# SSD stage of a decoder trunk: each group's scan placed between the half tiles of the following group's projection

## What is computed

```python
u = h @ w_in_a[l]                                     # z | x B C | dt
xbc, conv_new = causal_conv(u[..., D_INNER:D_INNER + CONV_DIM], ...)   # 4 taps, then silu
dt = softplus(dt_raw + dt_bias); A = -exp(a_log)
acum = cumsum(dt * A)                                 # within a chunk
decay_ls = exp(where(causal, acum[l] - acum[s], -inf))
cb = einsum('bclgn,bcsgn->bcgls', C, B)
y_diag = einsum('bcgrls,bcsgrp->bclgrp', cb * decay_ls, x * dt)
states = einsum('bclgn,bclgrp->bcgrpn', B, x * dt * decay_end)
# states are carried over the chunks: s = s * chunk_decay + states
y_off = einsum('bclgn,bcgrpn->bclgrp', C, prev) * exp(acum)
y = rmsnorm((y_diag + y_off + d_skip * x) * silu(z))
```

## Time and profile before

| what | value |
|---|---|
| median of three executions | 3522.46 us (3512.46 to 3524.99) |
| profiled execution | 3522.89 us, its span 3521.2 us |
| PE, DVE, ACT, POOL busy | 3233.1, 1475.4, 1153.1, 269.7 us |
| the chain that ended last | PE 88%, DVE 7%, ACT 2% |
| SSD groups (L1195 of the first to the end of the last) | 637 to 1228 us |

### The profile page before, as it was taken

One profiled execution on the slowest core, in us unless ns is written; L12 is line 12 of the kernel. 1 busy time (PEld: TensorE's weight loads), 2 busy tenths in 40 slices (PEclk: granted clock), 3 DMA queues, 4 the chain that ended last, 5 costly groups with the idle time before them and its releaser, 6 DMA issues.

```text
span 3521.2 us, 55459 instructions
## 1 busy us (share of the span) xinstructions
PE 3233.1 (92%) x22296; PEld 2958.1 (84%) x22296; DVE 1475.4 (42%) x2112; ACT 1153.1 (33%) x1615; POOL 269.7 (8%) x364
## 2 busy tenths in 40 slices
PE   6999996998888898998999999999897878899997
PEld 5899996777777786798999879999896666899996
DVE  4444325656565512325443344443432052444423
ACT  3433323433333332224332223332212242333322
POOL 0000000212221210000000000000001201100000
PEclk9999997999989998999999999999998997999998
DMA  6333221222222233322232233222331601223221
GB/s 199 123 89 89 86 87 53 74 70 66 62 62 62 74 97 108 114 84 66 83 89 89 73 107 103 86 86 88 97 90 38 233 27 51 67 86 87 88 88 52
DMA packets 444922, 305.93 MB, mean 87 GB/s; under 512 B 12517, under 2 KB 415645, under 8 KB 444701
## 3 DMA queue, kind: packets, MB, share of 16 engines
q1 hardware_dynamic: 421780, 231.03, 22.4%
q0 software_dynamic: 19744, 69.48, 5.8%
q10 hardware_dynamic: 3328, 4.47, 0.4%
HBM read 282.73 MB, written 22.20 MB: 87 GB/s over the span
## 4 chain that ended last, share of the span: by engine, by line
PE 88%; DVE 7%; ACT 2%; issue 1%; DMA 1%; ACTq 0%; POOL 0%; SPq 0%; DVEq 0%; POOLq 0%
PE PS L916 64%; PE PS L985 5%; PE PS L962 2%; PE PS L1107 2%; PE PS L1119 1%; PE PS L1236 1%; PE PS L1080 1%; PE PS L1058 1%; DVE yT L1430 1%; DVE rb L1415 1%; PE PS L1238 1%; PE PS L1097 1%; PE PS L1169 1%; PE PS L1248 1%; PE PS L1371 1%
## 5 line engine op out<-in xcount | busy, mean ns | idle before, releaser
L916 PE MATMUL PS<-hH,whi 128*128 128x272 f32 x4048 | 842.7, 289 | 16.4 <-DVE hL L1426 7.7
L916 PE MATMUL PS<-hH,wlo 128*128 128x272 f32 x4048 | 840.2, 289 | 0.0
L916 PE MATMUL PS<-hL,whi 128*128 128x272 f32 x4048 | 837.1, 288 | 0.0
L1411 DVE TENSOR_TENSOR wlo<-raw,whi 128x1024 fp32r<-128x1024 f32 (+2 forms) x401 | 488.8, 1219 | 794.9 <-ACT whi L510 787.4
L510 ACT ACTIVATE whi<-raw 128x1024 fp32r<-128x1024 f32 (+2 forms) x401 | 413.1, 1030 | 756.8 <-PE PS L916 669.2
L916 PEld LDWEIGHTS PS<-hH,whi 128*128 128x128 f32 x4048 | 639.7, 189 | 18.7 <-issue 17.1
L916 PEld LDWEIGHTS PS<-hL,whi 128*128 128x128 f32 x4048 | 639.0, 189 | 0.0
L916 PEld LDWEIGHTS PS<-hH,wlo 128*128 128x128 f32 x4048 | 634.3, 190 | 0.0
L916 PE MATMUL PS<-H,whi 128*128 128x272 f32 x1984 | 412.3, 289 | 5.8 <-DVE L L1817 2.5
L916 PE MATMUL PS<-H,wlo 128*128 128x272 f32 x1984 | 412.1, 289 | 0.0
L916 PE MATMUL PS<-L,whi 128*128 128x272 f32 x1984 | 410.4, 288 | 0.0
(11 more groups left out here) (323 smaller groups left out, 3536.9 us busy)
## 6 DMA issues: line engine op xcount, KB each, us to landing
raw<-in_w_ffn_gu SPq DMA_DIRECT2D x176, 512.0 KB, 3.7
kvr<-in_cache_mem_kv POOLq DMA_DIRECT2D x32, 1024.0 KB, 5.5
raw<-in_w_in_a SPq DMA_DIRECT2D x57, 512.0 KB, 3.7
raw<-in_w_ffn_down SPq DMA_DIRECT2D x64, 448.0 KB, 3.2
rawm<-in_w_mem_kv SPq DMA_DIRECT2D x32, 512.0 KB, 4.4
raw<-in_w_ffn_down SPq DMA_DIRECT2D x32, 512.0 KB, 3.4
raw<-in_w_out_a SPq DMA_DIRECT2D x24, 512.0 KB, 3.6
raw<-in_w_in_b SPq DMA_DIRECT2D x20, 512.0 KB, 3.6
```

What stands on the lines that cost most here:

```text
L916: mm = pe.matmul(PS[:, bank + h, 0:HT], w[:, slot, k * P:(k + 1) * P], x[:, h * HT:(h + 1) * HT], start=first and w is whi and x is hi_k, ...
L1411: dve.tensor_tensor(wlo[:, slot, 0:nk * P], src, whi[:, slot, 0:nk * P].bitcast(F32), ALU.subtract).then_inc(s["w_lo"], 1)
```

## The change

- Projection and scan get banks of their own: units use banks 0 and 1 (first and second half of the columns), the scan banks 2 to 7. A unit is now two half tiles of 24 matmuls (`half(g, j, h)`), each with its own full and free semaphores (`ph0`, `pf0`; `w_mm`, `pf1`).
- A period of group g runs units 4 and 5 of g and then the scan of g; between its steps stand the eight half tiles of units 0 to 3 of group g+1. ACT, DVE, POOL and SP have the work that belongs to them (evacuation, first tap, weight splits, taps, conv rows, loads) at matching places.
- The x, B and C tiles get a second set of buffers (`XB`), used by odd groups. The loop becomes: group 0, three turns of two groups, group 7 without a next one.
- Units 0 to 3 of group 0 stand around the dt chain on PE, DVE and ACT.
- A store of `nst` is awaited by DVE just ahead of the next use and not by POOL right behind the store. The scan has a single bank for the spread decays (before: two in turn), and the second new-state product stands behind head 3.
- Behind the loop PE waits for the last output sums (`y_read`) too.

The core of the diff:

```diff
+        XB = [[xbc[:, ti, :] for ti in range(4)], [rb[:, :], dtx_all[:, :], M1[:, 2 * NG - 2, :], M1[:, 2 * NG - 1, :]]]
...
+                    def half(g, j, h):
+                        if h == 0:
+                            pe.wait_ge(s["w_lo"], gx(g, 6, d.u0 + j + 3))
+                        pe.wait_ge((s["pf0"], s["pf1"])[h], gx(g, 6, j + 1))
+                        slot = (d.u0 + j) % 2
+                        for k in range(KD):
+                            for w, x in ((whi, hH), (whi, hL), (wlo, hH)):
+                                mm = pe.matmul(PS[:, h, 0:HT], w[:, slot, k * P:(k + 1) * P], x[:, k, h * HT:(h + 1) * HT],
+                                               start=k == 0 and w is whi and x is hH, stop=k == KD - 1 and w is wlo)
+                        mm.then_inc((s["ph0"], s["w_mm"])[h], 1)
...
-                            products((d.u0 + j) % 2, KD, 0, hH_of, hL_of, 2 * POS[j], True, True).then_inc(s["w_mm"], 1)
...
+                        ahead(0, 0)
                         spread(0)
...
+                        ahead(0, 1)
...
+                        state_rows(0)
+                        ahead(1, 0)
                         spread(1)
+                        ahead(1, 1)
                         head(0)
                         spread(2)
+                        ahead(2, 0)
                         head(1)
                         spread(3)
                         state_rows(1)
+                        ahead(2, 1)
...
                         new_states(0)
                         head(2)
+                        ahead(3, 0)
                         head(3)
...
+                        new_states(1)
+                        ahead(3, 1)
...
                         decay(0)
+                        ahead(0)
                         pair_decay(0)
                         state_rows(0)
                         decay(1)
+                        ahead(1)
                         pair_decay(1)
                         decay(2)
                         pair_decay(2)
                         decay(3)
                         state_rows(1)
+                        ahead(2)
                         pair_decay(3)
...
                         masked(0)
+                        if not last:
+                            conv(ahead, 0, st)
+                            history(ahead, 2)
                         seg(1)
+                        if not last:
+                            unit(g, 9)
                         masked(1)
                         seg(2)
+                        if not last:
+                            conv(ahead, 1, st)
+                            history(ahead, 3)
                         masked(2)
                         seg(3)
+                        if not last:
+                            unit(g, 10)
                         masked(3)
...
                         new_states(0)
+                        if not last:
+                            conv(ahead, 2, st)
                         new_states(1)
```

More of the change, by code:

```diff
@@ L1157, in _, with period, ahead @@
+                    for j in range(2, 4):
+                        half(0, j, 0)
+                        half(0, j, 1)
                     pe.wait_ge(s["hist_copied"], 1)
-                    d = ph["ssd"]
-                    e0 = list(n.ev)
-                    def group(g):
+                    pe.wait_ge(s["alb_sub"], 1)
+                    def period(g, last=False):
+                        xt = lambda ti: XB[parity(g)][ti]
+                        def ahead(j, h):
+                            if not last:
+                                half(following(g), j, h)
@@ L1788, in _ @@
[L1788 removed]
+                        assert last or st.n == VE, st.n
+                    periods(dve, period)
                     d = ph["qm", 0]
```

610 lines of the change are left out of this document (335 added, 275 removed).

## The result

The changed kernel takes 3425.3 us (median of four executions, 3424.1 to 3426.6); the kernel before took 3517.7 us beside it. The ratio is 0.9739, with a 95% interval of 0.972 to 0.9758. The profiled execution took 3424.1 us, with a span of 3422.4. The prediction was 3419, range 3410 to 3446.

What follows compares the result with a forecast made beforehand. PE was taken to bound the kernel, with idle or half-speed time to recover. Seven periods of 65.6 us, the opening and the last scan put the restart 104.7 us earlier: 3522.9 - 104.7 = 3418.2, stated as 3419, range 3410 to 3446.

Steps and rivals of the forecast that it cites:

- The period: Group loop: scan start to scan start takes 65.6 us instead of 78.5, from 64.7 + 0.2 + 0.7.
- The floor from rows at full clock: PE's shortest possible period: 36.2 us of projection tiles plus 28.5 us of scan work at full clock, 64.7 us.
- The changeovers: Sixteen new switches a period between half tiles and scan work on PE, priced at 0.7 us, between 0 and 2.6.
- the wait of the sixth tile: PE waits about 0.2 us a period around the sixth tile, until ACT's gate empties bank 0.
- T of group 0 at 611.2: T is the start of a group's fifth tile; group 0's was put at 611.2 us, after the dt chain.
- The wait of 1.7: PE's idle at the dt chain ahead of the groups falls from 10.92 us to about 1.7.
- The last scan: Group 7's scan, without tiles to hide behind: PE restarts 43.5 us after its start, before 45.0.
- The DVE cover: DVE's spare time before PE needs its masks: 2.2 us at the first head, 1.5 us at the second.
- POOL's contention: DVE's taps meet POOL's multiply of head 1: 0.75 to 1.05 us on DVE, nothing on PE, about 0.5 cover left.
- Rival 2: DVE late at the heads by 2 us a period beyond its cover: 14 us, 3433 (3440 at 3 us); chance 0.15.
- Rival 1: PE's clock falls inside each period, perhaps because transposes do not count: 15 us, 3434, or 3449 if twice; chance 0.15.
- Rivals 3 and 4: ACT and DVE stop PE at every tile, 3684, chance 0.03; waits eat the overlap to within 0.5%, chance 0.04.

Runs made afterwards that it cites:

- written-out kernel: All eight group-loop bodies of the changed kernel written out on every engine: 3406.2 us, ratio 0.9687 to the kernel before; in a later side-by-side timing 3398.6 us, 0.9662.
- the added steps: Loop written out, plus twelve dummy DVE steps ahead of the second head's differences: 3433.6 us, ratio 0.9775; with four such steps 3402.9 us, 0.9682.

## Why the prediction was right, and where it was not

**The period, 65.6 forecast.** It is 65.2 in five of seven. The floor from rows at full clock, 64.7, was right to 0.5; which step holds the 0.5 is open. The changeovers (0.7) and the wait of the sixth tile (0.2) did not show: PE has no idle there at all. The prediction took a mid value for the changeovers where the nearest row, a transpose behind a tile without idle, had said 0.

**The back edge, not in the sum.** This is the step that was missing: 5.8 us at each of two places, 11.6 in all. The change replaces one turn per group by one turn per two groups, and the prediction gave that nothing. The diff showed it; the trace of before could not show its cost, since its shorter turns stall nowhere. The runs show it from four sides: without any engine's back edge it is gone, with only PE's gone it is gone as well, the kernel before gets it as soon as its turn holds two groups, and at each stall three packets of PE's instruction queue come within 10 us, where the kernel before fetches none in its turns. No row names the fetch as the releaser, but PE goes on 1.4 to 1.7 us after a packet has landed, at all five back edges.

**The opening, T of group 0 at 611.2.** The wait of 1.7 is 1.19, and the dt transposes run at full clock, since PE was not idle before them: 1.8 us and not 3.1. The forecast's first scan stood at 611.2 + 12.3 = 623.5, 52.5 us behind the zero point of before (571.01); it starts at 619.26, 50.8 behind its own (568.51). So the opening was 1.7 us shorter than forecast.

**The last scan, 43.5 from its start to the restart.** It is 1130.04 - 1087.21 = 42.8, with the waits that were forecast: 1.93 ahead of the first head, 4.23 at its end.

**The sum.** Stage 98.4 us shorter instead of 104.7. The 6.3 us are: -1.7 for the opening, +11.6 for the back edges, -2.9 for seven periods of 65.2 instead of 65.6, -0.7 for the last scan. The forecast of 3419 was 6 us low because of one missing term of 11.6 and small ones that had been set too high. Two more things made the number come closer than the sum deserved. The stage's 98.4 us became 98.8 of the span only because the pieces behind it, which the prediction took as unchanged, moved by up to 6 us each way and cancelled. And the forecast was taken off the profiled execution, 3522.9; by the medians the change saved 3517.7 - 3425.3 = 92.4 us and not 104, since two of the four executions before took 3512 to 3513.

**The DVE cover.** The prediction had 2.2 us at the first head and 1.5 at the second, 0.5 of that left with POOL's contention. At the first head of the written-out kernel's second scan, in the prediction's time (the scan opens at T+12.3), the mask ends at T+31.1 (forecast 31.8) and PE comes at T+34.2 (34.0): 3.0 us spare. At the second head DVE ends the mask and PE takes it here:

```profile
710.32 0.67 DVE L1838 TENSOR_TENSOR Lh<-Lh,cbm 128x512 f32<-128x512 f32 x1
```

```profile
713.21 0.65 PE L1266 MATMUL PS<-Lh,xd 128*64 128x128 f32 x4
```

From the scan's opening at 685.16 the mask ends at 25.8 us, forecast 38.4 - 12.3 = 26.1 without contention, and PE comes at 28.1, forecast 39.9 - 12.3 = 27.6. So 2.2 us are spare, with the contention in it, and the added steps found 2.5. The contention is as priced. Two small taps of the same shape in the changed kernel, the second while POOL multiplies, differ by 1.05:

```profile
638.69 0.23 DVE L1726 SCALAR_TENSOR_TENSOR rb<-pres,cwg,rb 128x32 f32<-128x32 f32 x1
...
639.63 1.28 DVE L1726 SCALAR_TENSOR_TENSOR rb<-pres,cwg,rb 128x32 f32<-128x32 f32 x1
```

```profile
639.21 1.65 POOL L2151 TENSOR_TENSOR Eh<-Eh,xbc 128x512 f32<-128x512 f32 x1 [4.94 <-ACT Eh L828]
```

It did not eat the cover, because the rest of DVE's chain was a microsecond shorter than summed. It came more often than the one time priced: in the written-out kernel's second scan each of POOL's first three multiplies (694.44, 705.10, 711.25) overlaps one small DVE step of about 0.2 us, which then takes 1.27 to 1.36. Rival 2 needed 2 us more than the cover; no wait at a head shows in the periods.

**Rival 1, the clock.** Not in the changed kernel's periods: the clock falls only behind the two stalls. The reason given for it, that transposes do not count, is not borne out by the run with six times the transposes. A fall without idle exists all the same: in every written-out variant whose periods have no idle, but for that one, once or twice in seven periods, the clock stood at half for some 3 us and the period was 1.5 us longer. The windows of the written-out kernel at such a place:

```profile
994.00:996.00 2.00, 2.00 (x7) 0.79 (x6) 0.00 (x0) 0.67 (x2) 0.00 (x0) 1.00 0.00 0
996.00:998.00 2.00, 2.00 (x11) 1.96 (x11) 1.78 (x3) 0.00 (x0) 0.00 (x0) 0.65 0.00 0
998.00:1000.00 2.00, 2.00 (x10) 2.00 (x10) 1.93 (x6) 0.00 (x0) 1.60 (x2) 0.50 0.24 92
1000.00:1002.00 2.00, 2.00 (x18) 2.00 (x17) 0.78 (x2) 1.13 (x3) 0.00 (x0) 1.00 0.67 246
```

It stands some 42 us behind the small decays, behind the last head and the second new states' products (contraction over 32 rows), but in most periods the same work passes without it. What decides it is open.

**Rivals 3 and 4.** PE never waits for a bank or for split weights in the changed kernel's periods. The covers measured are those of DVE at the first two heads, 3.0 and 2.2 to 2.5 us; the others were not measured, but no wait shows that one was used up.

**Order against overlap.** The prediction did not part the gain. From zero point to restart, 109.2 us lie between the kernel before and the written-out one: 68.5 are the interleaving (1188.06 - 568.83 = 619.2 against 550.7), 15.3 the opening, and 26 the scan's new order and the banks (7 x 3.7). Each comes from one trace; together they make 109.8 and not 109.2.

## What to carry to other kernels

When a change makes a loop's body longer, put a term for the back edge into the sum: here a turn of one group cost nothing at it, a turn of two cost 4 us (kernel before) to 6 us (changed kernel), and writing the loop out removed it. Whether a body is fetched again each turn can be read beforehand: the kernel before has no instruction packet behind its first turn, each of the longer loops has nine or ten in a turn. Work put between dependent steps is worth the wait it covers plus the clock that the wait would have lowered, here as much again on average. And part a large gain by differences between rows that every variant has, for the time of the whole can move by 13 us for reasons that lie elsewhere.

## What was not expected of the hardware

- A long loop's back edge stalls TensorE: twice in the changed kernel, 1.6 and 2.3 us some 1.2 us apart, and once, for 2.0 to 2.4 us, in the kernel before with two groups a turn, with half clock behind it. Three instruction packets of 16 KB within 10 us go with each stall. Straight-line code of eight groups, fetched while it runs (22 instruction packets in 270 us), does not stall, and a turn of one group needs no fetch.
- A wait of 2.2 us in a busy stretch costs about 4.3 on average: 15 us of idle and 15 us of half clock in seven periods. The half clock's part lies between 0.1 and 4.8 us in a single period.
- 72 transposes in a row, 8.2 us of them, leave the clock at its upper level.
- The clock can fall without any idle, for 1.5 us of loss, at the same place of a period, in one or two of seven periods.
- An untouched stretch of 827 matmuls took 141.4, 148.0 or 154.3 us in different traces, with a granted clock of 0.92, 0.88 or 0.84.
